# Ten matmuls of ones at the start, one weight piece in two halves, and the front weights stored as one run per partition

## What is computed

```python
def reference(x, mem, ...):
    mix = hybrid_mixer(h, w_in, ..., w_out)     # one input projection (1024 -> 2824), window attention,
                                                # mLSTM recurrence, one output projection
    h = layer_norm(ALPHA * h + mix, ln1_g, ln1_b)
    ca = memory_cross_attention(h, mem, w_cq, w_ck, w_cv, w_co)   # 4 heads, 256 memory tokens
    h = layer_norm(ALPHA * h + ca, ln2_g, ln2_b)
    ff = moe_ffn(h, w_router, b_router, w_gu, b_gu, w_down, b_down)   # top 4 of 32 experts
    return layer_norm(ALPHA * h + ff, ln3_g, ln3_b)
```

## Time and profile before

| | us |
|---|---|
| median of 3 executions | 1201.1 (1200.85 to 1201.58) |
| the profiled execution's own time | 1200.45 |
| span of its trace (first to last instruction) | 1198.6 |
| TensorE busy | 1069.2 (89%) |
| VectorE / ScalarE / GpSimd busy | 359.8 / 159.4 / 32.6 |
| HBM read | 443.9 MB, 371 GB/s over the span |
| mean granted clock of TensorE | 0.962 |

### The profile page before, as it was taken

How to read it: one execution, slowest core, us unless ns; L and a number is a source line. 1 busy time by engine, 2 the same in 40 slices (tenths; PEclk the granted TensorE clock), 3 DMA queues, 4 the chain that set the end, 5 groups by cost and what they waited for, 6 DMA issues and landing times.

```text
span 1198.6 us, 20135 instructions
## 1 busy us (share of the span) xinstructions
PE 1069.2 (89%) x7918; PEld 460.9 (38%) x7919; DVE 359.8 (30%) x1195; ACT 159.4 (13%) x366; POOL 32.6 (3%) x27
## 2 busy tenths in 40 slices
PE   7999999999998858999986668999979969998975
PEld 6668646844332312333321113333323323333321
DVE  0714431226331311333321113333313313333314
ACT  0121100302110100111110001111101101111101
POOL 0520000001000000000000000000000000000000
PEclk9999999999999988999998889999999999999987
DMA  9973264647999999999999999999999999799995
GB/s 320 375 265 137 74 263 193 253 168 270 425 429 429 429 429 429 428 429 429 429 429 428 428 428 428 429 429 429 429 429 429 429 429 429 311 430 428 429 428 233
DMA packets 48784, 445.19 MB, mean 371 GB/s; under 512 B 5184, under 2 KB 6464, under 8 KB 23712
## 3 DMA queue, kind: packets, MB, share of 16 engines
q1 hardware_dynamic: 45872, 439.40, 88.2%
q10 hardware_dynamic: 2896, 5.57, 1.4%
HBM read 443.90 MB, written 1.05 MB: 371 GB/s over the span
## 4 chain that ended last, share of the span: by engine, by line
PE 65%; DMA 25%; SPq 6%; DVE 3%; issue 1%; ACT 0%; another core or an unknown queue 0%; DVEq 0%
PE bank L781 20%; DMA ring<-in_w_down 20%; PE bank L817 11%; PE bank L467 7%; PE bank L482 7%; PE bank L727 6%; SPq L351 5%; DMA ring<-in_w_gu 4%; PE bank L714 3%; PE bank L652 2%; PE bank L720 2%; PE bank L792 1%; DMA ring<-in_w_in 1%; PE bank L797 1%; PE bank L776 1%
## 5 line engine op out<-in xcount | busy, mean ns | idle before, releaser
L781 PE MATMUL bank<-ring,wk 128*32 128x512 f32 x3264 | 397.3, 635 | 86.4 <-DMA ring<-in_w_gu 86.4
L781 PEld LDWEIGHTS bank<-ring,wk 128*32 128x32 f32 x3264 | 105.5, 113 | 347.7 <-issue 215.3
L817 PE MATMUL bank<-ring,wk 128*32 128x512 f32 x1632 | 205.3, 595 | 0.0
L1409 DVE TENSOR_SCALAR wk<-bank 128x256 f32<-128x256 f32 x51 | 21.7, 425 | 565.5 <-PE bank L781 565.5
L727 PE MATMUL bank<-wk 64*128 64x512 f32 x416 | 105.4, 625 | 0.7 <-ACT wk L1005 0.7
L467 PE MATMUL bank<-ring 128*128 128x256 f32 x448 | 98.1, 380 | 4.3 <-issue 2.2
L467 PEld LDWEIGHTS bank<-ring 128*128 128x128 f32 x448 | 84.6, 190 | 16.5 <-issue 5.2
L817 PEld LDWEIGHTS bank<-ring,wk 128*32 128x32 f32 x1632 | 65.6, 109 | 64.1 <-issue 30.5
L997 ACT ACTIVATE wk<-wk 128x256 f32<-128x256 f32 x51 | 21.2, 417 | 479.6 <-DVE wk L1409 479.6
L482 PE MATMUL bank<-ring 128*128 128x512 f32 x192 | 83.0, 593 | 0.0
L727 PEld LDWEIGHTS bank<-wk 64*128 64x128 f32 x416 | 36.9, 192 | 75.8 <-issue 74.2
(11 more groups left out here) (286 smaller groups left out, 664.9 us busy)
## 6 DMA issues: line engine op xcount, KB each, us to landing
ring<-in_w_gu SPq DMA_DIRECT2D x128, 2048.0 KB, 32.6
ring<-in_w_down SPq DMA_DIRECT2D x64, 2048.0 KB, 38.5
ring<-in_w_in SPq DMA_DIRECT2D x5, 2048.0 KB, 20.9
ring<-in_w_ck SPq DMA_DIRECT2D x2, 2048.0 KB, 21.4
ring<-in_w_out SPq DMA_DIRECT2D x2, 2048.0 KB, 19.5
ring<-in_w_cv SPq DMA_DIRECT2D x2, 2048.0 KB, 7.8
ring<-in_w_cq SPq DMA_DIRECT2D x2, 2048.0 KB, 9.0
ring<-in_w_co SPq DMA_DIRECT2D x2, 2048.0 KB, 7.8
```

The costliest lines, as they stand in the source:

```text
L781: ins = mm(hidden(g), xg[:, kk, c, :], gate_and_up(w[:, kk, :], g), start=False, stop=2 * c + kk == KT - 1, skip_group_check=True)
L817: ins = mm(strip(7, 2 * d + b), actT[:, b, 2 * c + gg, :], wd[:, gg, b, 512 * d:512 * d + 512], start=c == 0 and gg == 0 and b == 1, stop= ...
```

## The change

Four things are edited.

1. GpSimd's memset of `ones` is the first of its memsets and signals `ones_set`. TensorE waits for it and issues ten matmuls of `ones` by `ones` (128 columns each) into bank 7 ahead of the unit "akav". Nobody reads their result.
2. The piece "mq" is loaded by two DMAs of 1 MB. Its layout is by column halves: the first half of the slot has columns 0 to 255 of all rows, the second the columns 256 to 511. The first half signals `mq_half`, the second `slot_landed[1]`. TensorE starts "mq" at `mq_half` and waits for `slot_landed[1]` ahead of its third group m.
3. All front pieces from "mq" on are laid out on the host in one array `w_front`, one block of 128 rows of 16 KB per piece, so that a DMA reads one run of 16 KB for each partition (8 KB for the halves of "mq"). The head, memT and all other inputs stay as they were.
4. `w_in`, `w_out`, `w_ck`, `w_cv`, `w_cq` and `w_co` are no inputs of the device program any more.

```diff
-                w, c0, width = SOURCE[piece]
                 s, _ = front_slot(piece)
-                sp.dma_start(slot_view(s, width), columns(w, c0, width)).then_inc(slot_landed[s], 16)
+                if piece == "mq":
+                    sp.dma_start(slot_words(s)[:, 0:half], w_front[n - 1, :, 0:half]).then_inc(mq_half, 16)
+                    sp.dma_start(slot_words(s)[:, half:SLOT], w_front[n - 1, :, half:SLOT]).then_inc(slot_landed[s], 16)
+                else:
+                    sp.dma_start(slot_words(s), w_front[n - 1]).then_inc(slot_landed[s], 16)
...
+            nc.gpsimd.memset(ones, 1.0).then_inc(ones_set, 1)
             nc.gpsimd.memset(av[0:CHUNK, 0, :], 0.0)
             nc.gpsimd.memset(akT[:, 0:CHUNK], 0.0)
-            nc.gpsimd.memset(ones, 1.0)
...
                 banks = open_unit(u)
-                w = landed(u)
+                halves = None
+                if u == "mq":
+                    pe.wait_ge(mq_half, 16)
+                    halves = slot_words(front_slot(u)[0]).rearrange("p (h k n) -> p h k n", h=2, k=KT)
+                else:
+                    w = landed(u)
                 for m in range(4):
+                    if halves is not None and m == 2:
+                        landed(u)
                     for k in range(KT):
-                        ins = mm(banks[m // 2][:, (m % 2) * 256:(m % 2) * 256 + 256], w[:, k, m * P:(m + 1) * P], rhs[:, k, :],
+                        cols = w[:, k, m * P:(m + 1) * P] if halves is None else halves[:, m // 2, k, (m % 2) * P:(m % 2) * P + P]
+                        ins = mm(banks[m // 2][:, (m % 2) * 256:(m % 2) * 256 + 256], cols, rhs[:, k, :],
...
+            pe.wait_ge(ones_set, 1)
+            for _ in range(10):
+                mm(psum[7][:, 0:P], ones, ones, start=True, stop=True)
             b0, b1 = open_unit("akav")
...
+    def piece_rows(name):
+        w = mixer[name] if name in mixer else square[name[:2]][:, 512 * int(name[2]):512 * int(name[2]) + 512]
+        if name == "mq":
+            return w.reshape(KT, P, 2, 256).transpose(1, 2, 0, 3).reshape(P, SLOT)
+        return w.reshape(KT, P, 512).transpose(1, 0, 2).reshape(P, SLOT)
+
+    w_front = np.stack([piece_rows(name) for name in PIECES[1:]])
```

21 lines of the change are left out of this document (7 added, 14 removed).

## The result

| | us |
|---|---|
| before, median of 20 | 1203.02 (1200.19 to 1205.71) |
| with the change, median of 20 | 1209.85 (1199.80 to 1217.83) |
| ratio | 1.0057, 95% interval 1.0039 to 1.0075 |
| forecast | 1198.2 (1196.5 to 1200.8), against 1201.1 for before |
| profiled execution with the change: own time, span, mean granted clock | 1215.74, 1213.9, 0.949 |

The change makes the kernel slower by 0.6%. The forecast had the wrong sign, and its range did not hold the time. The time with the change also scatters over 18 us, where before scatters over 5.5. One of its 20 executions (1217.83) is over 1.5% above the fastest and so counts as slow, though its granted clock is that of the others (0.956); with or without it the mean is 0.5 to 0.6% above before.

What follows compares the result with a forecast made beforehand. The experts' DMA stream sets the long stage's pace, and the front sets its start. "mq" 3.5 us earlier, less a new wait of about 0.6 for early, gives 2.9 us: 1198.2 against 1201.1, range 1196.5 to 1200.8.

Steps and rivals of the forecast that it cites:

- What bounds the kernel: Expert stage: its DMA stream at 427 GB/s sets the pace and starts behind the first pass, so the front's gain reaches the end.
- Ten matmuls: Front, ahead of "akav": 4.1 us of work in idle time raises the clock at no cost; "akav" ends at 13.1, not 14.67.
- Halves: Front: the first half of "mq" lands at 13.1 to 13.3, so TensorE starts it at 13.3, 3.5 us earlier.
- early_par and the issue of early: ScalarE's queue: early_par lands 3.4 us later beside larger packets, so early is issued at 20.8 rather than 17.43.
- Landing of early: ScalarE's queue: early lands at 28.0 against 23.7, a wait of about 0.6 us behind "mq", leaving 2.9 us gain.
- The bound that I had written: Landing of early: with all eight packets beside 16 KB packets it lands at 31.3, and the change loses 0.4 us.
- another case: Rival, expert stage: it takes the gain back; with the 0.4 us loss case 1201.1 to 1201.5, joint chance 0.10.
- Behind it, nothing: After early: late lands about 30 with nearly 4 us of cover, b_gu follows by as much, remaining pieces have slack: nothing.
- the slower one: Rival, ScalarE's queue starves: several q1 packets per q10 turn, early past 30.9, loss of 2.6 us, 1203.7; chance 0.08.
- The array isn't warm: Rival, front: clock still low at the head, "mq" starts at 14.8, or early lands at 29 or so: 1199.1; chance 0.12.

## Why the prediction was wrong, point by point

**What bounds the kernel** was right: the expert stage hands on the front's shift. It was +15.68 at the first pass and +15.3 at the end.

**Ten matmuls** in the changed kernel: nearly right (end of "akav" 13.61, I took 13.1). The head's first step was still at the low level and took 1.77 us rather than 0.89: the ten matmuls had worked for 4.6 us by then. The statement that they cost nothing was wrong on its own terms. Alone they cost 1.7 us, through the clock.

**Halves**: right. "mq" started at 13.62 against 13.3, a gain of 3.19 against 3.5.

**early_par and the issue of early**: the mechanism right, the term too small. `early_par` has eight packets for an engine, and each waits for one of 8 or 16 KB. I added 3.4 us and it was 4.8: it landed 10.7 us after its issue against 5.9 in the earlier trace rows, and the issue itself was 0.4 later. `early` was issued at 22.66 and not 20.8.

**Landing of early**: the step that failed. I took two packets beside mo and six beside memT, 28.0 us. Thirteen engines brought it at 28.4 to 29.2, but not by that sum: issued at 22.66, with no packet beside mo and eight beside memT, it is 22.66 + 6.3 - 0.24 = 28.7. An issue 1.9 us too early and two packets of mo too many nearly cancelled, which is luck. For the other three I had added up q1's bytes as if the 16 engines moved in step. They don't: memT's parts landed from 27.4 to 37.7 us, and a DMA has landed when its slowest engine has. The bound that I had written, 31.3 for eight packets beside 16 KB, was nearly that case (six of the eight and the signal behind them, on the last engine), but I took it for a loss of 0.4 us and gave it, with another case, 0.10. That case isn't rare: of 16 engines it is enough that one is ahead. And it was too low, since it stood on an issue at 20.8. From 22.66 the same working gives 22.66 + 6.3 + 4.2 = 33.2, and 34.5 was measured; three 16 KB packets that took 1.0 to 1.1 us while b_gu was read are the rest. That a load can halve the rate of all others stood in the trace of before (243 GB/s from 27 to 31 us) and is in no term of the prediction.

**Behind it, nothing**: the second step that failed, and the larger part of the loss. Of the 15.3 us the late landing itself, less the 3.2 gained at "mq", is 3.9. The rest came from what follows a wait: the clock at 0.50 after 6.95 us of idle time (3.3 us in the tiny matmuls and "mk"), again after the wait of 3.30 (1.8 us at 72), and for reasons not known at 246 and 294 us (1.4 and 1.8 us); and GpSimd's work on b_gu, pushed from 32 to 56 us and so onto VectorE's second pair of writes (3.3 us). I had followed `late` to the first pair only, with a landing at about 30 (it was 47.8, still in time for TensorE), and b_gu to nothing. Both stood in the trace of before: an array that starts at the low level after idle time in the earlier trace rows, and a pair of writes of 2.99 us in the earlier trace rows whose like takes 1.29.

**The rivals**: the slower one had the right place, ScalarE's queue, and the right point from which it decides (30.9). Its mechanism, several packets of q1 for each of q10, is refuted: 74 to 72. Its 0.08 was the only chance on the side that came. The Trainium skill's rule that an engine takes a packet of typically 9 to 17 descriptors before it turns (DMA: Bandwidth & Descriptors, Queues, rings and completion order) would have made it slower too; by the counts, with one run to a packet, the turns are one for one, and it is the size of one that does it. "The array isn't warm" came for the first step of eight only, and "mq" started at 13.62 all the same.

**The scatter** of 18 us: the kernel with memT behind mv scatters by 4, so that engines running ahead have a part in it is likely, but no execution of the changed kernel near 1200 us was profiled, and among the three that were (1209.9 to 1219.0) the landing of `early` differs by 1 us only. Those differ by what comes behind, VectorE beside GpSimd and the clock. Still open: why an engine is ahead; why b_gu's reads are slow; what lengthens some executions of the kernels with `early` first and with the tables on SyncE's queue (with b_gu moved too it is gone, which points to b_gu but doesn't show it); and why the clock falls for 3 us at 246 or 294 us in some executions and not in others; so whether the last 3 us of the loss belong to the change is open too.

## What to carry to other kernels

Two queues on the same engines take turns packet by packet, so longer runs on one make every small load on the other wait longer: `early_par`, eight packets for each engine, became 4.8 us slower. Before runs are lengthened, count the packets of what stands beside them and who waits for it; move those loads ahead or into the same queue, or keep the runs there at 2 or 8 KB. It can go the other way too: in the kernel with all tables on one queue it was the large load in 2 KB runs that came late beside x's 4 KB packets, though how much of that was the turns isn't shown. And a landing is that of the slowest of 16 engines, so price it by the worst neighbour that any engine may have, then follow a wait of several us on to the clock and to what comes late behind it.

## What the runs showed of the hardware

- Two hardware queues took turns one for one by packets, whatever their size: 66 to 64, 74 to 72, 107 to 103.
- The 16 engines can lie up to 10 us apart on one queue: the parts of memT landed from 27.4 to 37.7 us, those of `early` from 28.4 to 34.5.
- While b_gu's 8 KB packets were read, all DMA together moved 206 to 245 GB/s at a full busy share (424 in the same stretch without b_gu), and 16 KB packets took 1.0 to 1.1 us rather than 0.62.
- Idle times of TensorE of 2.77, 3.57 and 6.95 us were followed by a granted clock of 0.50 or 0.51, one of 2.15 us was not. The unit of 14.05 us behind them took 1.7 to 2.6 us longer.
- A VectorE tensor_tensor of 0.68 us took 4.55 beside a GpSimd tensor_tensor of 4.39.
- An engine that issues a DMA can stand still for long: ScalarE's issue of `ln_cols` lasted 36.51 us.
- 16 KB runs moved 427 GB/s against 386 for 2 KB. Against 2 KB runs they cost 0.9% of the time, 11 us, where small loads on the other queue were wanted early (1.0057 against 0.9967), and gained some 4 us where the tables and b_gu stood in the same queue (0.9967 against 0.9999).
